# A three-block transformer on one core: order of work in the recurrence, at two gates and in the convolution

## What is computed

```python
def gla_chunk_scan(q, k, v, g):          # block 1, 8 heads, once forward and once backward in time
    # per chunk, G = cumsum(g):
        q_dec = qi * jnp.exp(G)
        k_inv = ki * jnp.exp(-G)
        k_end = ki * jnp.exp(G_last - G)
        attn = jnp.where(mask, jnp.einsum('bhik,bhjk->bhij', q_dec, k_inv), 0.0)
        o = (jnp.einsum('bhij,bhjv->bhiv', attn, vi)
             + jnp.einsum('bhik,bhkv->bhiv', q_dec, state))
        new_state = (jnp.exp(G_last[..., 0, :])[..., None] * state
                     + jnp.einsum('bhjk,bhjv->bhkv', k_end, vi))
# hgrn2_mixer:    return (rms_norm(o_f + o_b) * jax.nn.silu(gate)) @ w_out
# first_block, for each of two layers (mixer: hgrn2, then latent attention):
        h = h + rms_norm(m, post_mix_norm[i])
        f = squared_relu_mlp(rms_norm(h, pre_mlp_norm[i]), w_mlp_in[i], w_mlp_out[i])
        h = h + rms_norm(f, post_mlp_norm[i])
        e = p[i].astype(h.dtype) @ w_ple_proj[i]
        g = jax.nn.sigmoid(h @ w_ple_gate[i])
        h = h + rms_norm(g * e, ple_norm[i])
# second_block: hybrid_mixer (differential attention of 4 heads beside a causal convolution
# of 31 taps over 512 channels), cross_attention over 256 memory tokens, conv_ffn.
```

## Time and profile before

| | |
|---|---|
| median of 3 runs | 2334.65 us (2334.12 to 2335.09) |
| the profiled execution | 2332.7 us |
| its span, first to last instruction | 2330.9 us |
| busy: PE, POOL, DVE, ACT | 98%, 67%, 55%, 28% |
| mean granted clock of TensorE | 0.995 |
| chain that ended last | PE 91%, DVE 5%, POOL 3%, ACT 1% |

### The profile page before, as it was taken

One profiled execution on the slowest core, in us unless ns is written; L12 is line 12 of the kernel. 1 busy time (PEld: TensorE's weight loads), 2 busy tenths in 40 slices (PEclk: granted clock), 3 DMA queues, 4 the chain that ended last, 5 costly groups with the idle time before them and its releaser, 6 DMA issues.

```text
span 2330.9 us, 27596 instructions
## 1 busy us (share of the span) xinstructions
PE 2280.3 (98%) x10430; PEld 1855.1 (80%) x10430; DVE 1282.2 (55%) x1825; ACT 653.0 (28%) x1202; POOL 1568.7 (67%) x1532
## 2 busy tenths in 40 slices
PE   8999999999999899999999999999999999999998
PEld 6888877888887688888778888787668788888887
DVE  7774737245245777175544364469865445626354
ACT  3443433101013455154311010132344232202113
POOL 8556557877776654644497777678426947878784
PEclk9999999999999999999999999999999999999999
DMA  5222222333332211211243333333212422333332
GB/s 170 77 73 82 72 82 77 109 99 95 100 95 77 72 38 32 81 41 54 69 121 106 96 110 103 95 87 109 64 37 77 122 56 94 99 96 96 99 95 77
DMA packets 112725, 200.16 MB, mean 86 GB/s; under 512 B 12496, under 2 KB 21200, under 8 KB 112592
## 3 DMA queue, kind: packets, MB, share of 16 engines
q1 hardware_dynamic: 109424, 194.72, 29.0%
q10 hardware_dynamic: 3168, 3.67, 0.5%
HBM read 196.24 MB, written 2.10 MB: 85 GB/s over the span
## 4 chain that ended last, share of the span: by engine, by line
PE 91%; DVE 5%; POOL 3%; ACT 1%; issue 0%; DMA 0%; SPq 0%; DVEq 0%; POOLq 0%
PE bank L479 26%; PE bank L481 26%; PE bank L480 26%; POOL wL L2777 2%; PE bank L916 1%; DVE bank L1936 1%; DVE h L1928 1%; POOL wH L2775 1%; PE bank L1040 1%; DVE aL L1936 1%; PE bank L512 1%; PE bank L885 1%; PE bank L887 1%; PE bank L886 1%; PE bank L893 1%; PE bank L894 1%
## 5 line engine op out<-in xcount | busy, mean ns | idle before, releaser
L2777 POOL TENSOR_TENSOR wL<-raw,wH 128x512 fp32r<-128x512 f32 (+2 forms) x732 | 1002.9, 1370 | 61.1
L2775 POOL TENSOR_SCALAR wH<-raw 128x512 fp32r<-128x512 f32 (+2 forms) x732 | 530.0, 724 | 587.3 <-PE bank L481 496.8
L479 PE MATMUL bank<-aH,wH 128*128 128x512 f32 x1376 | 546.5, 397 | 12.7 <-DVE aL L1936 7.0
L481 PE MATMUL bank<-aH,wL 128*128 128x512 f32 x1376 | 536.6, 390 | 0.0
L480 PE MATMUL bank<-aL,wH 128*128 128x512 f32 x1376 | 536.5, 390 | 0.0
L479 PE MATMUL bank<-uH,wH 128*128 128x512 f32 (+1 forms) x978 | 378.4, 387 | 0.0
L481 PE MATMUL bank<-uH,wL 128*128 128x512 f32 (+1 forms) x978 | 376.8, 385 | 0.0
L480 PE MATMUL bank<-uL,wH 128*128 128x512 f32 (+1 forms) x978 | 376.8, 385 | 0.0
L479 PEld LDWEIGHTS bank<-aH,wH 128*128 128x128 f32 x1376 | 258.4, 188 | 73.3 <-POOL wL L2777 13.8
L480 PEld LDWEIGHTS bank<-aL,wH 128*128 128x128 f32 x1376 | 258.6, 188 | 56.5 <-issue 4.1
L481 PEld LDWEIGHTS bank<-aH,wL 128*128 128x128 f32 x1376 | 258.4, 188 | 54.7
(11 more groups left out here) (328 smaller groups left out, 3208.9 us busy)
## 6 DMA issues: line engine op xcount, KB each, us to landing
raw<-in_ws SPq DMA_DIRECT2D x698, 256.0 KB, 2.6
raw<-in_ws SPq DMA_DIRECT2D x24, 192.0 KB, 2.3
h<-in_xT SPq DMA_DIRECT2D x8, 256.0 KB, 5.5
E<-in_memT ACTq DMA_DIRECT2D x16, 128.0 KB, 2.7
raw<-in_ws SPq DMA_DIRECT2D x10, 128.0 KB, 2.2
tmp<-in_pT ACTq DMA_DIRECT2D x4, 256.0 KB, 3.2
out<-c_F SPq DMA_DIRECT2D x2, 512.0 KB, 2.9
out<-c_F SPq DMA_DIRECT2D x2, 384.0 KB, 2.9
```

The lines of the kernel that those rows point to most:

```text
L479: P.e.matmul(o, lH, rH, start=start, stop=False, skip_group_check=skip)
L481: return P.e.matmul(o, lL, rH, start=False, stop=stop, skip_group_check=skip)
L2775: G.e.tensor_scalar(H, x, 1.0, 0.0, MUL, ADD).then_inc(*G.did("wH", n))
L2777: G.e.tensor_tensor(L, x, H.bitcast(F32), SUB).then_inc(*G.did("w", n))
```

## The change

It changes the order of work on PE, ACT and DVE in five places; the instructions, their operands, the list of the weights, POOL's and SP's queues stay as they are, but for one square that moves from DVE to ACT.

- PE makes the query projection of head 0 ahead of the sum of squares.
- PE's `recur` makes the transposes of both directions, then the scores of both, then the state products of both.
- In the last head ACT and DVE do `recur` ahead of the output gate.
- The square of the eighth tile of the gated embedding is made by ACT in both layers, ahead of its table load, and DVE's is gone. In layer 1 both halves of the memory keys stand behind the sum.
- `d_normed` is cut in two; in the loop over heads 0 and 1 the low part comes behind the low parts of `d_turned(hd + 1)`. For heads 2 and 3 the order is what it was.

```diff
--- before.py
+++ after.py
@@ -511,7 +511,7 @@
                 P.wait_ge(cs_in)
                 i = P.e.matmul(b.ap[:, 0:n], ones, sums[:, 0:n], start=True, stop=not tail)
                 if tail:
-                    P.wait_ge(V if sid[0] == "ple" else A, "sq", sid, tiles - 1)
+                    P.wait_ge(A, "sq", sid, tiles - 1)
                     i = P.e.matmul(b.ap[:, 0:n], ones, sq[:, 0:n], start=False, stop=True)
                 i.then_inc(*P.did("stat", *sid))
                 if adds:
@@ -634,6 +634,7 @@
                         i = P.e.transpose(b.ap[:, cols128(n)], g_ke[d][:, cols128(n)], ident)
                     i.then_inc(*P.did("keT", head, d))
                     give(b, A, "kT", head, d)
+                for d in range(2):
                     b = take("S", head, d)
                     P.wait_ge(V, "ki", head, d)
                     P.wait_ge(V, "qd", head, d)
@@ -676,9 +678,9 @@
 
             project(0, 1)
             project(0, 2)
+            project(0, 0)
             stat_end("a1")
-            for part in (0, 3):
-                project(0, part)
+            project(0, 3)
             project_v(0)
             columns("a1")
             for head in range(8):
@@ -792,12 +794,11 @@
                 for o in range(3, 8):
                     linear(("gate", i, o), (A, "sg", i, o), "w_ple_gate", i, 128 * o, aH, aL, hs_ready)
                 P.also("gate done", i)
-                if i == 1:
-                    memory_keys(0)
                 stat_end("ple", i, adds=f"n{i}")
                 P.also("end ple", i)
                 if i == 1:
-                    memory_keys(2)
+                    for o in (0, 2):
+                        memory_keys(o)
                 P.wait_ge(A, "end ple", i)
                 P.wait_ge(V, "end ple", i)
                 lin = three_open(keys_next, events_next)
@@ -1402,12 +1403,14 @@
                     out_gated(head - 1)
                 if head < 7:
                     sigmoid_f(head + 1, 0)
-                sigmoid_g(head)
                 if head < 7:
+                    sigmoid_g(head)
                     sigmoid_f(head + 1, 1)
+                    recur(head)
                 else:
+                    recur(head)
+                    sigmoid_g(head)
                     exp_table()
-                recur(head)
                 if head < 7:
                     for d in range(2):
                         log_f(head + 1, d)
@@ -1523,11 +1526,9 @@
                     if o > 1:
                         A.wait_ge(V, "Fg", i, o - 2)
                     do(mr[o % 2][:, :], bk("gate", i, o)[:, :], ACT.Sigmoid).then_inc(*A.did("sg", i, o))
-                    if o < 7:
-                        A.wait_ge(V, "Fg", i, o)
-                        square(("ple", i), o, F[:, o, :])
+                    A.wait_ge(V, "Fg", i, o)
+                    square(("ple", i), o, F[:, o, :])
                 exp_table()
-                squares_end[1] = (P, "stat", "ple", i)
                 A.also("end ple", i)
                 A.wait_ge(P, "end ple", i)
                 A.wait_ge(V, "end ple", i)
@@ -2110,11 +2111,14 @@
                 if head < 7:
                     project_f(head + 1, 0)
                     key_gate(head + 1, 0)
-                out_gate(head)
                 if head < 7:
+                    out_gate(head)
                     project_f(head + 1, 1)
                     key_gate(head + 1, 1)
-                recur(head)
+                    recur(head)
+                else:
+                    recur(head)
+                    out_gate(head)
                 if head < 7:
                     for d in range(2):
                         log_decay(head + 1, d)
@@ -2255,9 +2259,6 @@
                     tt(F[:, o, :], E[:, o, :], mr[o % 2][:, :], MUL).then_inc(*V.did("Fg", i, o))
                     if 0 < o < 7:
                         add_squares(("ple", i), o)
-                V.wait_ge(V, "Fg", i, 7)
-                V.wait_ge(V, "sum", ("ple", i), 6)
-                tt(sq[:, :], F[:, 7, :], F[:, 7, :], MUL).then_inc(*V.did("sq", ("ple", i), 7))
                 V.also("end ple", i)
                 V.wait_ge(P, "end ple", i)
                 V.wait_ge(A, "end ple", i)
@@ -2543,9 +2544,11 @@
                 V.wait_ge(A, "rstd", "dn", hd)
                 V.wait_ge(V, *(("rr", 2 * hd + 4) if hd < 2 else ("y2L", hd - 1)))
                 stt(y, bk("do", hd)[:, :], lam[:, 5:6], root("dn", hd), MUL, MUL).then_inc(*V.did("dn", hd))
+
+            def d_normed_low(hd):
                 V.wait_ge(V, "dn", hd)
                 V.wait_ge(A, "y2H", hd)
-                low(uL[:, hd, :], y, uH[:, hd, :]).then_inc(*V.did("y2L", hd))
+                low(uL[:, hd, :], tmp[0][:, :], uH[:, hd, :]).then_inc(*V.did("y2L", hd))
 
             some_taps(27)
             for t in range(4):
@@ -2587,6 +2590,7 @@
                     ts(d_acc[:, BY_PE, :], bk("ctap")[:, :], vv("cv_dw_b_2", BY_PE), None, ADD, None).then_inc(*V.did("conv", BY_PE))
                 d_normed(hd)
                 d_turned(hd + 1)
+                d_normed_low(hd)
             V.wait_ge(P, "mu")
             for i in range(4):
                 V.wait_ge(*((V, "conv", i) if i == BY_PE else (A, "conv", i)))
@@ -2608,6 +2612,7 @@
                 stt(d_acc[:, i, :], d_acc[:, i, :], vv("cv_ln_g_2", i), root("ln"), MUL, MUL).then_inc(*V.did("lnn", i))
             d_turned(3)
             d_normed(2)
+            d_normed_low(2)
 
             def convolved_low(i):
                 V.wait_ge(A, "y2H", 4 + i)
@@ -2616,6 +2621,7 @@
             convolved_low(0)
             convolved_low(1)
             d_normed(3)
+            d_normed_low(3)
             convolved_low(2)
             convolved_low(3)
             xvalues(0)
```

## The result

The changed kernel took 2314.75 us (median of 4 runs, 2314.08 to 2315.66) against 2334.39 (4 runs, 2332.36 to 2335.09) for the kernel before beside it: a ratio of 0.9918, with a 95% interval of 0.99 to 0.9935. The forecast was 2316.6, and 2314.7 for the profiled execution, which took 2314.11.

What follows compares the result with a forecast made beforehand. PE, busy 2280.3 of 2330.9 us, was taken as the bound. Gains 1.4 + 6.6 + 5.9 + 0.9 - 0.4 + 3.65 = 18.05 us gave 2314.7 profiled, 2316.6 median; range 2314 to 2319.5, chance 0.71.

Steps and rivals of the forecast that it cites:

- Start: First sum of squares: query projection ahead covers PE's wait for DVE's last partial sum; gain 1.4 us, bounds 0.9 to 1.5.
- Heads 0 to 6: Recurrence: PE's new order removes the wait for the first g_kT copy, 0.94 us a head; gain 6.6 us.
- Head 7: Last head's recurrence: the 3.99 us g_kT wait and the half clock behind it go; gain 5.9 us.
- Layer 0 square: Gated embedding, layer 0: ACT makes the last square faster than DVE, so the logarithm starts sooner; gain 0.9 us.
- Layer 1: Square on ACT, memory keys behind the sum: POOL's third weight tile and PE come later; loss 0.4 us.
- Convolution: Low part moved behind the four: PE loses 1.95 us of idle time and 1.7 of half clock; gain 3.65 us.
- rival (d): Recurrence, all heads: late g_ke or g_qd of the second direction holds the first's product; slower, 2340.6 us at 3 a head; chance 0.02.
- Rival (b): Recurrence: something other than the copy releases the state products, so heads 0 to 6 give nothing; 2323.2 us; chance 0.07.
- rival (c): Layer 0's table load is paid twice, another 1.28 us: loss 0.3 instead of gain 0.9; 2317.8 us; chance 0.04.
- Rival (a): Clock does not come back: head 7 or convolution keeps its half clock, layer 1 loses 2; 2321.6 us; chance 0.13.
- From the span to the median: Whole kernel: the median was put about 2 us above the profiled execution, 2316.6 against 2314.7 us.

Runs made afterwards that it cites:

- e10_start: The kernel before with only the third projection of head 0 put ahead of the first sum of squares; 2330.55 us.
- e1_order: The kernel before with only PE's new order in the recurrence (both directions' keys, then scores, then products); 2322.14 us.
- e2: The kernel before with only the last head's states ahead of its gate on ACT and DVE; 2329.71 us.
- e4_squares: The kernel before with only the eighth square on ACT in both layers, the memory keys where they were; 2332.99 us.
- e5_again: The changed kernel once more, unaltered; 2314.43 us, ratio 0.9918.
- e3_conv: The kernel before with only d_normed cut in two, its low part behind the four low parts; 2331.68 us.
- e8_table: The changed kernel with ACT's logarithm table load ahead of the eighth square instead of behind it; 2314.47 us.
- e7_piece7: The changed kernel with POOL preparing one more weight piece before its stop behind each layer's x and n; 2310.39 us, ratio 0.9905.
- e9_keys: The kernel before with only layer 1's first memory keys put behind the sum, the eighth square kept on DVE; 2334.67 us.

## Why the prediction was right, and where it was not

| Term | predicted | step in the changed kernel | the edit alone |
|---|---|---|---|
| Start | 1.4 | 1.49 | 1.49 (e10_start) |
| Heads 0 to 6 | 6.6 | 6.31 | 6.31 (e1_order) |
| Head 7 | 5.9 | 5.80 | 2.70 and 4.90 (e1, e2) |
| Layer 0 square | 0.9 | 0.84 | 0.88 (e4_squares) |
| Layer 1 | -0.4 | 0.96; -0.64 in e5_again | 1.11 and 0.92 (e4, e9) |
| Convolution | 3.65 | 3.70 | 3.71 (e3_conv) |
| Sum | 18.05 | 19.10 | |

The inputs came 0.6 us later than in the profiled execution of before, so 18.6 of the 19.1 reached the span (a drift of 0.1 is spread over the rest). That 2314.11 lies so near to the 2314.7 forecast for a profiled execution is in part luck: 1.36 too little for layer 1 stands against 0.3 too much for heads 0 to 6 and 0.6 of later inputs, and e5_again's, with the half clock, took 2315.21. In layer 1 both single edits are counted with no half clock behind the third tile.

*Start*: right, and it was counted from a pitch, which is why it stood. ACT read the sum at 30.89 and not near 29, behind another constant that DVE wrote later than before; nothing on PE moved by it, as assumed.

*Heads 0 to 6*: the mechanism is right. The size was 0.94 a head and is 0.90: the three blocks take 3.70, not 2 x 1.82. The condition of rival (d) did not arise: no row of PE's waits names g_ke or g_qd. Rival (b) falls with it.

*Head 7*: the step is right to 0.1, but it hangs on two edits, which the text had in one term. The prediction's first copy, ready some 0.4 us ahead of need, was ready 0.5 ahead (284.35 to 284.83).

*Layer 0*: right. The rows decide on the price of the load: 1.28 us, and the next instruction 0.01 behind, in the changed kernel and in e8_table, with ACT computing right up to the load in both. That is rival (c) refuted, and with it, for this case, the 2.66 us by which the Trainium skill ("ScalarE: Activation LUTs", What ACT_TABLE_LOAD costs) would have made this edit a loss of 0.4. The page splits it into a load of about 1283 ns, which the trace bears out, and a drain of about 1380, of which these rows show nothing.

*Layer 1*: this is the term that failed. Its first half holds: POOL's third tile was said to be 0.4 later, by two more slow pieces and one fewer at 0.44 each, and it is 0.37 later (19.52 to 19.89). The failed half is "I take a loss of 0.4", which carried the half clock over from before unchanged. The profiled execution had none, which the text had as its other bound, a gain of 1.0. The prediction took a property of one execution of before for one of the place. Like for like, with a half clock in both, the step is a loss of 0.64: POOL's 0.37, and 0.3 since in before the stretch began 0.6 us ahead of the restart and so was partly idle.

*Convolution*: right, but 1.7 of the 3.65 are clock, and they were there to be gained only in some executions of before. How the clock stood behind each wait, in all profiled executions that have it:

| Place and wait | us at clock 0.50 |
|---|---|
| Head 7, 3.99 to 4.00 | 3.4 (before, e3, e9, e10), 6.8 (e4) |
| Head 7, 2.87 | none (e1) |
| Layer 0, 3.8 to 3.9 | 6.8 (before, after, e4, e5, e7 to e10), 10.2 (e1 to e3) |
| Layer 1, 1.65 and 1.65 (1.5 in e4, 1.2 in e2) | 3.4 (before, e1, e3, e10), 6.8 (e2), none (e4) |
| Layer 1, 2.42 for the square | 3.4, over the memory keys (e9) |
| Layer 1, after the change, 0.8 and 1.64 | none (after, e7, e8), 3.4 (e5) |
| Convolution, 1.99 | 3.4 (before, e4), none (e1, e10), 6.8 (e2, e9) |

*From the span to the median*: the prediction added 2 us, because before's median stood 2 above its profiled execution. For the changed kernel it is 0.6. This is most of the miss of 1.85 us (the rest is layer 1's 1.36, less 0.6 of arrival and 0.3 of the other terms). The likely reason, argued and not tested, is that two of the places where executions differ, head 7 and the convolution, are gone; all executions of before spread over 6.5 us (2330.7 to 2337.22), those of the changed kernel over 2.3. The granted clock on record for each speaks for it: 0.996 in the fastest of before (2330.7), 0.994 in the slowest (2337.22), 0.997 or 0.998 in all of the changed kernel. Rival (a) had it the wrong way round: it let the clock's loss stay in head 7 and the convolution where the wait went, and no profiled execution showed that.

## What to carry to other kernels

Size an edit by the shift of one matmul ahead of it and one behind it; that gave every term but layer 1 the same within 0.1 us in both profiled executions of the changed kernel, where single times of the kernel before differed by up to 6. It takes out the arrival of the inputs, but not the clock: where a step is larger than its wait, read the granted clock of both traces first. If a stretch at the half clock follows a wait, count its gain as what it costs on average over executions, not as what one trace shows, and shrink the spread too when the wait goes. And before spending on the clock, look at who is next: here 2.8 us won back in layer 0 were lost within 16 us to DVE's low parts and POOL's weights, until POOL prepared one piece more ahead of its stop; then 1.4 stayed.

## What the hardware showed that was not expected

The same wait at the same place (1.99 us in the convolution, in kernels that are alike there) was followed by 0, 3.4 or 6.8 us at the lower level of 1.2 GHz, and one of 3.8 in layer 0 by 6.8 or 10.2; in two executions of one kernel the wait of 1.65 in layer 1 was followed by 0 and 3.4; one such stretch of 3.4 us cost 1.60 us of time where PE was busy all through it, while of a stretch of 6.8 us that began 3.2 us before PE had work only 3.63 us were busy, and 1.2 us less were lost than with 6.05 busy (e7_piece7). POOL and DVE slow each other in a locked rhythm: either of POOL's two instructions can be the one that pays, 0.62 to 1.06 (changed kernel) or 1.29 to 1.61 (e9_keys), and the piece costs 2.39 or 2.28 us accordingly.
